# First and last norms reordered, gathers split, last weight chunk in halves, in a one-core fp32 encoder layer

## What is computed

```
h = rms_norm(x, mix_norm);  proj = h @ w_in                      # 1024 -> 7184 columns
y_a = sgu_branch(proj[u|v]);  y_b = mamba2_branch(proj[z|xbc|dt])
x = x + (sigmoid(g_a) * (y_a @ Wa) + sigmoid(g_b) * (y_b @ Wb)) @ w_out
x = x + moe_ffn(rms_norm(x, ffn_norm))                           # top-4 of 32 experts, clamped SwiGLU
x = x + sigmoid(rms_norm(x, ple_norm) @ Wg) * (p @ Wp)
return rms_norm(x, final_norm)
```

## Time and profile before

| | |
|---|---|
| median of 3 runs | 1229.29 us (1228.64 to 1230.97) |
| profiled execution, its own time | 1227.98 us |
| its span | 1226.2 us |
| PE busy | 1167.1 us (95%) |
| DVE, ACT, POOL busy | 394.3, 224.8, 45.1 us |
| moved by DMA | 459.60 MB, mean 375 GB/s |

### The profile page before, as it was taken

The page is one execution under the profiler, slowest core; times in us unless marked ns, Lnnn a source line. Parts: engine busy times, 40 slices in busy tenths (PEclk is TensorE's granted clock), DMA queues, the critical chain, the costliest instruction groups (busy, mean ns, idle before and its releaser), DMA issues.

```text
span 1226.2 us, 14127 instructions
## 1 busy us (share of the span) xinstructions
PE 1167.1 (95%) x5773; PEld 586.7 (48%) x5773; DVE 394.3 (32%) x716; ACT 224.8 (18%) x338; POOL 45.1 (4%) x32
## 2 busy tenths in 40 slices
PE   9999999999999999999998989899999999999997
PEld 8988888874343443434332423233343333233336
DVE  2679954653221232122121212212222121212127
ACT  5766654350000000000000000000000000000017
POOL 6600000010000000000000000000000000000000
PEclk9999999999999999999999999999999999999999
DMA  8655478789999999999999999999999999999991
GB/s 271 203 172 206 137 275 334 266 304 403 430 427 427 429 428 428 429 428 428 429 428 429 430 429 428 429 426 428 427 427 428 428 428 428 429 428 427 428 391 46
DMA packets 62382, 459.60 MB, mean 375 GB/s; under 512 B 7385, under 2 KB 16993, under 8 KB 37506
## 3 DMA queue, kind: packets, MB, share of 16 engines
q1 hardware_dynamic: 62338, 458.95, 91.0%
HBM read 457.87 MB, written 1.06 MB: 374 GB/s over the span
## 4 chain that ended last, share of the span: by engine, by line
PE 68%; DMA 27%; DVE 2%; ACT 2%; issue 1%; ACTq 0%; SPq 0%; DVEq 0%
PE bank L1032 22%; DMA wring<-in_w_dram 15%; PE bank L1070 13%; DMA vz<-in_w_dram 12%; PE bank L712 5%; PE bank L714 5%; PE bank L713 5%; PE bank L993 4%; PE bank L1002 3%; PE bank L1038 2%; PE bank L777 1%; PE bank L782 1%; PE bank L787 1%; PE bank L699 1%; PE bank L1061 1%
## 5 line engine op out<-in xcount | busy, mean ns | idle before, releaser
L1032 PE MATMUL bank<-wring,hT 128*64 128x512 f32 x1360 | 310.4, 599 | 21.0 <-DMA wring<-in_w_dram 17.5
L1032 PEld LDWEIGHTS bank<-wring,hT 128*64 128x64 f32 x1360 | 94.1, 137 | 210.6 <-issue 171.9
L1985 DVE TENSOR_SCALAR xbcT<-bank 128x512 f32<-128x512 f32 x32 | 22.1, 692 | 526.4 <-PE bank L1038 526.4
L1070 PE MATMUL bank<-wring,xbcT 128*64 128x512 f32 x672 | 150.7, 595 | 7.3 <-DVE xbcT L2004 6.3
L1494 ACT ACTIVATE xbcT<-xbcT 128x512 f32<-128x512 f32 x32 | 20.2, 630 | 489.3 <-DVE xbcT L1985 489.3
L1070 PEld LDWEIGHTS bank<-wring,xbcT 128*64 128x64 f32 x672 | 46.5, 137 | 101.4 <-issue 91.7
L1632 DVE TENSOR_TENSOR blk_lo<-blk,blk_hi 128x2048 fp32r<-128x2048 f32 x32 | 73.0, 2287 | 39.5 <-ACT blk_hi L1309 39.5
L1032 PE MATMUL bank<-vz,hT 128*64 128x512 f32 x336 | 78.7, 599 | 7.1 <-DMA vz<-in_w_dram 7.1
L1499 ACT ACTIVATE xbcT<-bank 128x512 f32<-128x512 f32 x31 | 18.5, 597 | 352.5 <-PE bank L1070 352.5
L1032 PE MATMUL bank<-blk,hT 128*64 128x512 f32 x352 | 79.7, 594 | 3.2 <-DMA blk<-in_w_dram 3.2
L1070 PE MATMUL bank<-blk,xbcT 128*64 128x512 f32 x320 | 72.6, 595 | 3.1 <-DVE xbcT L2004 3.1
(11 more groups left out here) (300 smaller groups left out, 1215.2 us busy)
## 6 DMA issues: line engine op xcount, KB each, us to landing
wring<-in_w_dram SPq DMA_DIRECT2D x129, 2048.0 KB, 36.0
blk<-in_w_dram SPq DMA_DIRECT2D x42, 2048.0 KB, 35.5
vz<-in_w_dram SPq DMA_DIRECT2D x21, 2048.0 KB, 35.9
blk<-in_w_in_dram SPq DMA_DIRECT2D x28, 1024.0 KB, 5.2
blk<-in_w_branch_a_dram SPq DMA_DIRECT2D x4, 1024.0 KB, 5.5
blk<-in_w_branch_b_dram SPq DMA_DIRECT2D x4, 1024.0 KB, 8.1
blk<-in_w_out_dram SPq DMA_DIRECT2D x4, 1024.0 KB, 5.2
x<-in_x_dram SPq DMA_DIRECT2D x4, 512.0 KB, 5.3
```

The source lines that it names most:

```text
L1032: last = mm(bank[dh * SLOTS:(dh + 1) * SLOTS, :], xgT[:, k, :], at(c)[:, kk * 2 * F + off + dh * W:kk * 2 * F + off + (dh + 1) * W], start ...
L1070: last = mm(YB[dh * SLOTS:(dh + 1) * SLOTS, :], units[:, kk * P + c * SLOTS:kk * P + (c + 1) * SLOTS], at(W1C + c)[:, kk * D + dh * W:kk * ...
L1985: ts(g_sb, GLU[:, :], LIMIT, None, ALU.min).then_inc(g_done, 1)
```

## The change

**Head.** The gain row is spread over the 128 partitions by its load (512 KB written), and this load stands between those of x's two tiles. The two spreading products go; the idle products are twelve in a row. The first norm reads x from the memory of `ga`, so ACT copies the high part of each transposed block as soon as it is there. DVE makes the first block's rest between the two tiles' products.

**First expert.** Its rows are gathered in two halves into two banks, with a wait for `gateT_done` ahead (one of the banks held that matrix), and PE starts on the first half when it is there.

**Last two experts.** The gather for expert 31 goes between the chunks of w1 of expert 30. w2 of expert 31 goes to bank LIN, and its first chunk is used ahead of the scatter of expert 30. The last chunk is loaded as two halves.

**Last norm.** Tile 0's root is taken once its own squares are there, which puts a table load ahead of the fifth sigmoid; another brings the sigmoid's table back, and a third the root's again. Tile 0 is written and stored ahead of tile 1.

```diff
+        mix_gain = z[:, 0, :]
+        x_first = ga
...
-            load(mix_row, mix_norm, mix_loaded)
             for t in range(TT):
-                load(x[:, t, :], x_in[0, t * P:(t + 1) * P, :], x_loaded[t])
+                load(x_first[:, t, :], x_in[0, t * P:(t + 1) * P, :], x_loaded[t])
+                if t == 0:
+                    load(mix_gain, vec(mix_norm), mix_loaded)
...
+                elif g < NCH * E - 1:
+                    load(slots[g % NSLOT], chunk_src(*LAST_TWO[g - NCH * (E - 2)]), loaded[g % NSLOT])
                 else:
-                    load(slots[g % NSLOT], chunk_src(*LAST_TWO[g - NCH * (E - 2)]), loaded[g % NSLOT])
+                    for k in range(2):
+                        part = slice(k * RW2 // 2 * D, (k + 1) * RW2 // 2 * D)
+                        load(slots[g % NSLOT][:, part], chunk_src(E - 1, NCH - 1)[:, part], last_half[k])
...
-            keep_busy(idle_bank, 6, halves[:], halves[:])
+            keep_busy(idle_bank, 12, halves[:], halves[:])
             pe.wait_ge(consts, 2)
-            pe.wait_ge(mix_loaded, 16)
-            for h in range(HALVES):
-                last = mm(banks[(6 + h + BANK_SHIFT) % BANKS][:, :], ones[0:1, :], mix_row[:, h * W:(h + 1) * W], start=True, stop=True)
-            last.then_inc(gain_spread, 1)
-            keep_busy(idle_bank, 6, halves[:], halves[:])
...
-                pe.wait_ge(xg_done, j + 1 + (not alone and side == 1))
+                if first:
+                    pe.wait_ge(first_rows, 2)
+                else:
+                    pe.wait_ge(xg_done, j + 1 + (not alone and side == 1))
...
+                    if first and RW1 * c == KT // 2:
+                        pe.wait_ge(xg_done, 1)
...
-                units_of(first, *stream(first), 0)
-                gather(last_chosen)
+                def rows_between(c):
+
+                    gather(last_chosen if c == 0 else lambda: None, range(2 * c, 2 * c + 2))
+
+                units_of(first, *stream(first), 0, between=rows_between)
+                gather(lambda: None, range(6, KT))
...
                 rows_out(actT, *stream(first), between=second_turned)
-                pe.wait_ge(y_copied, first + 1)
-                scatter(lambda: None)
-                selected(GLU)
+                def first_scattered(c):
+
+                    pe.wait_ge(y_copied, first + 1)
+                    scatter(lambda: None)
+                    selected(GLU)
+
                 pe.wait_ge(actT_done, second + 1)
-                rows_out(actT_last, *stream(second))
+                rows_out(actT_last, *stream(second), between=first_scattered, to=LIN, halved=True)
...
+                pe.wait_ge(gateT_done, 1)
...
-            gather(first_ready)
+            first_ready()
+            for h, bank in enumerate((YB, TB)):
+                for k in range(4):
+                    for t in range(TT):
+                        last = mm(bank[:, k * SLOTS:(k + 1) * SLOTS], xp[:, t, (4 * h + k) * P:(4 * h + k + 1) * P],
+                                  sel[t][:, 0:SLOTS], start=(t == 0), stop=(t == TT - 1))
+                last.then_inc(first_rows if h == 0 else gathered, 1)
...
-            split(0, [0])
-            act.wait_ge(xn_done, 2 * TT)
-            high_parts("xT", a_hi)
+            for t in range(TT):
+                for h in range(2):
+                    if (t, h) == (1, 1):
+                        split(0, [0])
+                    name = ("xT", t, h)
+                    wait_filled(act, name)
+                    fn(a_hi[:, 4 * h:4 * h + 4, t * P:(t + 1) * P], seg4(bank_of(name)[:, :]), ACT.Copy).then_inc(act_high, 1)
...
-            take_y(E - 1)
+            act.wait_ge(chunk_used, NCH * E)
+            fn(y_sb, LIN[:, :], ACT.Copy).then_inc(y_copied, 1)
...
             square(0, 0, W, 0, 1)
+            sigmoid(0, W, W, 3, banks[2])
             square(1, 0, W, 0, 2)
-            sigmoid(0, W, W, 3, banks[2])
             square(0, W, W, 1, 3)
             sigmoid(1, W, W // 2, 4, banks[3])
-            square(1, W, W // 2, 1, 4)
-            sigmoid(1, W + W // 2, W // 2, 5, banks[4])
             fn(table_out[:, 6:7], ones[:, 0:1], ACT.Sqrt)
             root(0, 1)
-            square(1, W + W // 2, W // 2, 2, 5)
-            root(1, 2)
+            fn(table_out[:, 7:8], ones[:, 0:1], ACT.Sigmoid)
...
+            sigmoid(1, W + W // 2, W // 2, 5, banks[4])
+            fn(table_out[:, 0:1], ones[:, 0:1], ACT.Sqrt)
+            square(1, W, W // 2, 1, 4)
+            left_half(0)
+            square(1, W + W // 2, W // 2, 2, 5)
+            root(1, 2)
+            left_half(1)
...
-            dve.wait_ge(gain_spread, 1)
+            dve.wait_ge(mix_loaded, 16)
             for t in range(TT):
+                if t:
+                    first_low(0)
                 dve.wait_ge(root_done, t + 1)
...
-                    stt(v[:, t, cols], x[:, t, cols], rstd[:, t:t + 1], banks[(6 + h + BANK_SHIFT) % BANKS][:, :], ALU.mult,
+                    stt(v[:, t, cols], x_first[:, t, cols], rstd[:, t:t + 1], mix_gain[:, cols], ALU.mult,
                         ALU.mult).then_inc(xn_done, 1)
-            low_parts("xT", a_hi, a_lo, 0)
+            for n in range(1, 4):
+                first_low(n)
...
             embedded(0, 0, W, 1)
             embedded(1, 0, W, 2)
+            embedded(0, W, W, 3)
+            dve.wait_ge(x3_sq, 2)
+            ts(part3[:, 0:1], ssq3[:, 0, 0:1], 1.0 / D, RMS_EPS, ALU.mult, ALU.add).then_inc(x3_part, 1)
...
+            rooted(0)
+            embedded(1, W + W // 2, W // 2, 5)
+            dve.wait_ge(x3_sq, 4)
+            link(tt(part3[:, 1:2], ssq3[:, 1, 0:1], ssq3[:, 1, 1:2], ALU.add))
+            ts(part3[:, 1:2], part3[:, 1:2], 1.0 / D, RMS_EPS, ALU.mult, ALU.add).then_inc(x3_part, 1)
+            rooted(1)
```

More of the change, by code:

```diff
@@ L256, in build @@
         ssm_gain = xc[:, 3072:4096].rearrange("p (g n) -> p g n", g=GROUPS)
-        mix_row = z[0:1, 0, :]
+        mix_gain = z[:, 0, :]
+        x_first = ga
         fnorm = slots[7][:, 0:D]
@@ L320, in build @@
         mix_loaded = sem("mix_loaded")
-        gain_spread = sem("gain_spread")
+        first_rows = sem("first_rows")
+        last_half = [sem(f"last_half{k}") for k in range(2)]
         ssm_loaded = sem("ssm_loaded")
@@ L1062, in turned_units, with rows_out @@
                 last.then_inc(actT_filled, 1)
-            def rows_out(units, at, arrived, between=None):
+            def rows_out(units, at, arrived, between=None, to=YB, halved=False):
                 for c in range(W2C):
-                    arrived(W1C + c)
+                    if not (halved and c):
+                        arrived(W1C + c)
                     for kk in range(RW2):
+                        if halved and c and kk % 2 == 0:
+                            pe.wait_ge(last_half[kk // 2], 16)
                         for dh in range(2):
-                            last = mm(YB[dh * SLOTS:(dh + 1) * SLOTS, :], units[:, kk * P + c * SLOTS:kk * P + (c + 1) * SLOTS],
+                            last = mm(to[dh * SLOTS:(dh + 1) * SLOTS, :], units[:, kk * P + c * SLOTS:kk * P + (c + 1) * SLOTS],
                                       at(W1C + c)[:, kk * D + dh * W:kk * D + (dh + 1) * W],
@@ L1314, in _ @@
                 act.wait_ge(x_loaded[t], 16)
-                fn(u[:, t, :], x[:, t, :], ACT.Square, accum_out=ssq[:, t:t + 1]).then_inc(ssq_done, 1)
+                fn(u[:, t, :], x_first[:, t, :], ACT.Square, accum_out=ssq[:, t:t + 1]).then_inc(ssq_done, 1)
                 act.wait_ge(ssq_done, t + 1)
@@ L1573, in _, with left_half @@
             square(0, 0, W, 0, 1)
+            sigmoid(0, W, W, 3, banks[2])
             square(1, 0, W, 0, 2)
-            sigmoid(0, W, W, 3, banks[2])
             square(0, W, W, 1, 3)
             sigmoid(1, W, W // 2, 4, banks[3])
-            square(1, W, W // 2, 1, 4)
-            sigmoid(1, W + W // 2, W // 2, 5, banks[4])
             fn(table_out[:, 6:7], ones[:, 0:1], ACT.Sqrt)
             root(0, 1)
-            square(1, W + W // 2, W // 2, 2, 5)
-            root(1, 2)
-            for t in range(TT):
+            fn(table_out[:, 7:8], ones[:, 0:1], ACT.Sigmoid)
+            def left_half(t):
                 act.wait_ge(x3_rstd, t + 1)
@@ L1635, in _, with first_low @@
             tt(dsel[:, :], ident[0:2 * HEADS, 0:HEADS], ident[0:2 * HEADS, HEADS:2 * HEADS], ALU.add).then_inc(small_set, 1)
-            dve.wait_ge(gain_spread, 1)
+            def first_low(n):
+                t, h = divmod(n, 2)
+                dve.wait_ge(act_high, n + 1)
+                cols = (slice(None), slice(4 * h, 4 * h + 4), slice(t * P, (t + 1) * P))
+                name = ("xT", t, h)
+                tt(a_lo[cols], seg4(bank_of(name)[:, :]), a_hi[cols].bitcast(FP32), ALU.subtract).then_inc(empty(name), 1)
+            dve.wait_ge(mix_loaded, 16)
             for t in range(TT):
+                if t:
+                    first_low(0)
```

(11 more changed lines are left out.)

## The result

The changed kernel takes **1231.78 us** (median of 20 runs, 1230.45 to 1233.35), the kernel before 1228.86 (median of 20, 1225.92 to 1231.18): ratio 1.0023, 95% interval 1.0016 to 1.0029. It is 2.9 us slower. The forecast was 1231.4 with a range of 1228.2 to 1233.5, and 0.55 on a time within 0.2%, 0.37 on slower. The measured 0.23% lies just over that bound, and its interval holds the bound.

A forecast was written before the change was run, and what follows sets the result against it. PE's chain was taken to bound the head and first expert, the stream of expert weights what follows; -0.5 + 1.7 - 0.5 + 0.3 + 1.1 = +2.1 on the 1229.29 median gave 1231.4 us, range 1228.2 to 1233.5.

The forecast's parts named there:

- Head, the arrival: Head: x's second tile lands at about 7.2, so the projection starts at 14.2 instead of 14.71: -0.5 us.
- no wait, by 0.4: Head: POOL's first rest ends at 16.0 and PE wants it at 16.4, so PE does not wait.
- Head, the clock: Head: PE's idle stretches of 2.1 to 2.7 and 1.5 us lose the clock, slowing the projection: +1.7 us.
- rival 2: Head: the clock stays low in the projection for two spells, +3.4 instead of +1.7, 1233.1 us; chance 0.18.
- rival 1: Head: the clock holds, as twelve idle products may lift it early; +0.4 in all, 1229.7 us; chance 0.22.
- First expert: First expert: the split gather saves the 0.83 wait for scaling, a new wait costs 0.3: -0.5 us.
- All of it kept: First expert: the whole -0.5 us reaches the end, since chunk 9's issue moves with it.
- Last experts: Last two experts: PE waits 1.2 us for a landing where it waited 0.7 for a copy: +0.3 us.
- Last norm: Last norm: two more table switches cost more than tile 0's early stores win: +1.1 us.
- Rival 3: Last norm: each of the two added table switches costs 1.4 us more, 1234.2 us; chance 0.05.
- rival 4: Whole kernel, faster: second tile by 6.3 (-1.2), clock held, first expert -0.8, norm +0.3: 1227.6 us; chance 0.07.
- the forecast's own spread: Whole kernel: about 1 us each way around the forecast, a third of it above 1231.8 and counted as slower.

The follow-up runs named there:

- run 5: The changed kernel with nine idle products behind the first tile's transposes and four behind the second's: 1229.72 us, ratio 1.0011 to the kernel before.
- run 10: The kernel before with the new head, eleven idle products in PE's idle stretches and the first weight half's high part made earlier: 1229.66 us, ratio 1.0004.
- run 1: The kernel before with the head's part of the change alone: 1230.99 us, ratio 1.0022.
- run 6: The changed kernel with ten idle products where PE waits for expert 30's SwiGLU: 1231.90 us, ratio 1.0034 to the kernel before.
- run 7: The changed kernel with the last norm of the kernel before put back: 1231.29 us, ratio 1.0027 to the kernel before.
- run 8: The changed kernel with expert 29's scatter ahead of the transposes of expert 30: 1231.84 us, ratio 1.0032 to the kernel before.
- run 3: The kernel before with the last two experts' part of the change alone: 1229.30 us, ratio 1.0005.
- run 9: The kernel before with three idle products between the first expert's gather and its first product: 1228.59 us, ratio 0.9997.
- run 4: The kernel before with the last norm's part of the change alone: 1229.42 us, ratio 1.0002.
- run 2: The kernel before with the first expert's split gather alone: 1227.58 us, ratio 0.9989.
- run 12: The kernel before with the split gather alone, its wait for the copied gate matrix ahead of the second half only: 1228.32 us, ratio 0.9993.

## Why the prediction was right, and where not

**The sum.** +2.1 predicted, +2.9 measured, and the largest term was the one named as deciding. That the forecast of 1231.4 is within 0.4 of the time is in part luck: 0.4 of it comes from the base, 1229.29 by three runs where twenty have 1228.86, and too much taken off at the first expert and too much added at the last norm cancel in part.

**Head, the arrival: -0.5 predicted, 0 measured.** The landing worked out from bytes was too early: 5.7 for the gain and 7.2 for the second tile were 6.43 and 7.87. The 7.0 behind it was too long: with the clock held it is 6.4 (7.84 to 14.21, run 5). The two errors cancel, so that run 5 starts at the predicted 14.2 is luck. In the changed kernel 0.5 us more went at the lower clock, in the transposes above all. And the step "no wait, by 0.4" looked at POOL's first rest alone; the second one holds PE and takes the 0.5 (run 5). So even the predicted arrival was worth nothing (runs 5, 10).

**Head, the clock: +1.7 predicted, about +2.4 measured.** The mechanism was right: idle stretches as named (2.72 and 1.26 against 2.1 to 2.7 and 1.5), then a low clock. The size was one spell by the earlier trace rows, and it was nearer to rival 2: low from 10.3 to 20.5, 5.8 us of it in the projection. Rival 2 had this with +3.4. The pair of traces gives 2.5, the means over the profiles 2.4, and holding the clock gives back 1.6 to 2.1 by the medians. The first half of rival 1 did happen: the twelve idle products had lifted the clock by 7.53, where eight transposes take 1.23, and the idle stretch lost it again (1.97 for the next eight). The clock did not hold in any profile of the new head with no idle products in those stretches (after and runs 1, 6, 7, 8).

**First expert: -0.5 predicted.** The start is right to the hundredth. "All of it kept" failed as far as the profiles can tell: from chunk 6's issue to the gate's it is 914.79 against 914.76, 914.3 to 915.4 over the eight profiles with the split gather, and with the old one 914.3 to 914.8 in four (before and runs 1, 3, 9), 915.9 in run 10 and 916.8 in run 4. Why the earlier start is not kept, while the low spell of run 4 seems to be, stays open. Alone it was 1.2 faster by the median (run 2), of which the spread, and not the start, is the better reading; 0.6 in run 12.

**Last experts: +0.3 predicted,** and 0.2 to 0.3 measured against six profiles of the old order, 0.8 against that of before, with the mechanism as written. The landing is hardly ahead of SP's issue (1181.22 and 1181.29 in run 3), not by up to 0.5 as was allowed; what brings the term down is that the 8.83 of before, which it was taken from, is 9.4 in other executions. The low clock ahead of the scatter was not predicted. It is covered by the stream (runs 6, 8), as the prediction said of all PE time saved at this place.

**Last norm: +1.1 predicted, +0.7 in the profile.** The last store is 1.0 later (1.2 predicted), and the shorter queue gives 0.3 of it back. The profiles of runs 4 and 7 have the same 0.6. Two separate timings, +0.7 and +0.5 by medians, agree without proving it.

**Rival 3 falls.** From the end of the fourth sigmoid (1219.37) to the root at 1220.79 it is 1.42 us, table load and its small activation among it; the other two switches look alike. The Trainium skill (ScalarE: Activation LUTs, What ACT_TABLE_LOAD costs) has 2.66 with the draining. Its 1.28 for the load agrees with all three rows, and its further 1.38 is not in this trace.

**The chances.** The time fell inside the range and 0.4 from the forecast, but past the 0.2% bound of the kernel before as measured now, in the third of the forecast's own spread that was counted as slower. The 0.08 on faster was more than rival 4's 0.07, though rival 4 itself was within 0.2%.

## What to carry to other kernels

A change that brings data earlier can lose more by the idle stretches it leaves on TensorE than it wins, so price each new one by the products behind it at half rate, or fill it with idle products. Before counting an early start, follow the other inputs of the same products (here POOL's second rest and the weight halves): if they stand where they stood, so does the end. When a gain is near the spread of the runs, look at the whole list of times: a stall that happens in a third of them is hardly in the median.

## What the runs showed that I had not expected

- An idle stretch does not cost the clock each time. Ahead of the transposes of expert 30 PE idles 1.83 us in run 3 as in the changed kernel; the four transposes behind it take 0.63 in the one and 1.09 in the other. What decides it is open.
- The load that spreads 4 KB over 128 partitions held up the tile behind it by at least 1.55 us (its square starts at 7.87 instead of 6.32, where it did not wait), against the 1.4 by bytes.
- 1.6 us of TensorE's time saved inside the saturated stream moved nothing (run 6), and 0.5 at its first expert nothing that a profile shows. A low spell of 1.7 at the first expert seems to have been carried (run 4, 916.83).
- The start of the old head is not the same in every execution either. Its first product starts at 14.7 to 14.9 in the profiles of before and runs 2, 3 and 9, at 14.29 in run 4 and at 14.00 in run 12, where the 16 transposes ahead of it take 2.54 instead of 3.36.
